# A hybrid decoder step on one core: the place of a weight split, the order and places of filler matmuls, and the reload of x

## What is computed

```
h = rms_norm(x); u = h @ w_in                       # RWKV, attention and gate columns
o_r = rwkv_time_mix(u_r); o_f = forgetting_attention(u_f)
merged = sigmoid(g_r) * (o_r @ w_br_rwkv) + sigmoid(g_f) * (o_f @ w_br_fox)
x = x + merged @ w_out
h2 = rms_norm(x); x = x + square(relu(h2 @ w_up)) @ w_down
y = rms_norm(x)
```

```
state = state * w_t - (state @ kk_t) (kk_t * a_t)^T + v_t k_t^T ;  y_t = state @ r_t
```

## Time and profile before

| what | us |
|---|---|
| median of 3 runs | 2137.5 |
| lowest and highest of these | 2125.45, 2142.78 |
| the profiled execution | 2131.06 |
| its span, first to last instruction | 2129.2 |
| PE busy in the span | 2043.7 (96%) |

### The profile page before, as it was taken

How to read it: one execution, slowest core, us unless ns; L and a number is a source line. 1 busy time by engine, 2 the same in 40 slices (tenths; PEclk the granted TensorE clock), 3 DMA queues, 4 the chain that set the end, 5 groups by cost and what they waited for, 6 DMA issues and landing times.

```text
span 2129.2 us, 43171 instructions
## 1 busy us (share of the span) xinstructions
PE 2043.7 (96%) x17718; PEld 1836.3 (86%) x17718; DVE 943.1 (44%) x1507; ACT 617.1 (29%) x997; POOL 194.6 (9%) x186
## 2 busy tenths in 40 slices
PE   7999989999999999998899999999999999999997
PEld 7996678888888887665566999999999999999997
DVE  6557554444444454607685753332123222222334
ACT  5015332322232222214354642322022012202313
POOL 0000222222222222001110000000000000000000
PEclk9999999999999999999999999999999999999999
DMA  4214621111222202746644561111111111111112
GB/s 168 89 30 167 203 54 44 43 33 45 54 64 74 73 29 75 187 98 251 204 157 162 190 223 47 40 50 49 40 50 40 50 45 43 49 39 50 41 48 81
DMA packets 112938, 185.36 MB, mean 87 GB/s; under 512 B 65198, under 2 KB 68590, under 8 KB 111238
## 3 DMA queue, kind: packets, MB, share of 16 engines
q1 hardware_dynamic: 110502, 174.91, 26.2%
q10 hardware_dynamic: 2304, 8.50, 1.5%
HBM read 147.71 MB, written 35.67 MB: 86 GB/s over the span
## 4 chain that ended last, share of the span: by engine, by line
PE 84%; DVE 6%; DMA 4%; SPq 2%; issue 2%; ACT 1%; ACTq 0%; DVEq 0%
PE ps L292 47%; PE ps L385 10%; PE ps L996 4%; PE ps L997 3%; PE ps L381 3%; PE ps L382 2%; PE ps L383 2%; DMA weights<-in_wu 1%; PE ps L1027 1%; SPq L805 1%; DVE arena L1870 1%; PE ps L872 1%; DMA normed<-in_vp 1%; DVE arena L2036 1%; PE ps L1239 1%
## 5 line engine op out<-in xcount | busy, mean ns | idle before, releaser
L292 PE MATMUL ps<-h_high,wb_split 128*128 128x350 f32 x1536 | 290.5, 324 | 0.0
L292 PE MATMUL ps<-ff_high,wb_split 128*128 128x350 f32 x1488 | 281.0, 323 | 0.0
L302 ACT CAST wb_split<-weights 128x1024 fp32r<-128x1024 f32 x88 | 92.1, 1046 | 600.6 <-PE ps L292 592.9
L292 PEld LDWEIGHTS ps<-h_high,wb_split 128*128 128x128 f32 x1536 | 254.7, 189 | 0.4
L292 PEld LDWEIGHTS ps<-ff_high,wb_split 128*128 128x128 f32 x1488 | 247.2, 189 | 0.0
L385 PE MATMUL ps<-normed,weights 128*128 128x350 f32 x696 | 229.1, 477 | 0.0
L385 PEld LDWEIGHTS ps<-normed,weights 128*128 128x128 f32 x696 | 130.3, 194 | 67.7 <-issue 7.3
L2194 DVE TENSOR_TENSOR arena<-arena,ps 128x1050 f32 (+1 forms) x39 | 48.7, 1249 | 314.1 <-PE ps L292 314.1
L2277 POOL TENSOR_TENSOR arena<-arena,constants 64x512 f32<-64x512 f32 x120 | 132.7, 1106 | 386.9 <-DVE arena L1870 325.9
L292 PE MATMUL ps<-ff_low,wb_split 128*128 128x350 f32 x744 | 160.3, 323 | 0.0
L996 PEld LDWEIGHTS ps<-arena 64*64 64x64 f32 x2400 | 145.0, 135 | 16.7 <-issue 15.7
(11 more groups left out here) (329 smaller groups left out, 3406.8 us busy)
## 6 DMA issues: line engine op xcount, KB each, us to landing
weights<-in_wu SPq DMA_DIRECT2D x122, 512.0 KB, 3.5
normed<-in_vp SPq DMA_DIRECT2D x64, 260.0 KB, 4.7
normed<-in_kp SPq DMA_DIRECT2D x64, 256.0 KB, 5.6
arena<-chunk_dram SPq DMA_DIRECT2D x10, 1248.0 KB, 6.9
arena<-gate_dram SPq DMA_DIRECT2D x16, 525.0 KB, 4.1
chunk_dram<-arena SPq DMA_DIRECT2D x12, 520.0 KB, 5.0
chunk_dram<-fox SPq DMA_DIRECT2D x12, 520.0 KB, 4.6
arena<-samp_dram SPq DMA_DIRECT2D x10, 512.0 KB, 9.5
```

The source lines that it names most:

```text
L292: last = pe.matmul(PS[:, 3 * s + g, 0:G], ws[s][wh][:, k * P:(k + 1) * P], tile_of(x[xh], k)[:, g * G:(g + 1) * G], start=(k == 0 and wh + ...
L302: act.copy(of[0][s][0], W[:, s]).then_inc(w_hi[s], 1)
```

## The change

There are three edits. First, in a chunk DVE makes the second side's low weights behind the four masks, where they stood ahead of them. Second, the fillers change in order and place: in every second group (those with an odd number, from chunk 1 on) the 8 tiles run in the opposite order, so 5 to 0 and then 7 and 6, and the first matmul of a group opens the accumulation whichever tile it is; the four fillers that stood behind both rounds of products become two behind each round. Third, SP fetches x in 8 DMAs of one tile, each behind the two gate tiles of a pass of the branch loop, where it was one DMA behind the loop; DVE waits for all eight.

```diff
--- before.py
+++ after.py
@@ -359,8 +359,9 @@
 
             def __init__(self, pe, v, ns=0, first=None):
                 self.pe, self.v, self.ns, self.first = pe, v, ns, first
-                late = [*range(NS, KT), *range(NS)] if ns or first else range(KT)
-                self.left = [(s, g, i, k) for s in range(2) for g in range(NG) for i, k in enumerate(late)]
+                late = [*range(NS, KT), *range(NS)] if ns or first else list(range(KT))
+                self.left = [(s, g, i, k) for s in range(2) for g in range(NG)
+                             for i, k in enumerate(late[::-1] if ns and (NG * s + g) % 2 else late)]
 
             def run(self, n=None):
                 for s, g, i, k in self.left[:n]:
@@ -378,7 +379,7 @@
                     out, w = PS[:, 6 + m % 2, 0:G], W[:, s, k * P:(k + 1) * P]
                     if k < self.ns:
                         wl_ = WL[:, s, k * P:(k + 1) * P]
-                        self.pe.matmul(out, fill_w(s, k), HF[:, k, at], start=False, stop=False)
+                        self.pe.matmul(out, fill_w(s, k), HF[:, k, at], start=(i == 0), stop=False)
                         self.pe.matmul(out, fill_w(s, k), HL[:, k, at], start=False, stop=False)
                         last = self.pe.matmul(out, wl_, HF[:, k, at], start=False, stop=(i == KT - 1))
                     else:
@@ -840,16 +841,24 @@
             reload(V_BR0 + 1, 0)
             sp.wait_ge(da_step, 11)
             sp.wait_ge(o_done, 2)
+            def x_tile(n):
+                sp.dma_start(XT[:, n, :] if isinstance(n, int) else
+                             XT[:, bass.ds(n, 1), :].rearrange("p o n -> p (o n)"),
+                             A["xt"][:, n, :] if isinstance(n, int) else
+                             A["xt"][:, bass.ds(n, 1), :].rearrange("p o n -> p (o n)")).then_inc(x_back, 16)
+
             gates_back(0)
             reload(V_BR0 + 1, 1)
+            x_tile(0)
             sp.wait_ge(sg_ready, 2)
             gates_back(1)
+            x_tile(1)
             with sp.Fori(2, KT) as n:
                 reload(n + V_BR0, 0)
                 reload(n + V_BR0, 1)
                 sp.wait_ge(sg_ready, 2 * n)
                 gates_back(n)
-            sp.dma_start(XT, A["xt"]).then_inc(x_back, 16)
+                x_tile(n)
             with sp.Fori(V_OUT0, PAIRS) as v:
                 for s in range(2):
                     reload(v, s)
@@ -1028,8 +1037,8 @@
                                                  AR[rows, p].rearrange("p a b -> p (a b)"), start=True,
                                                  stop=True)
                         ch_pe.done(last, f"prod_{m}{i}")
-
-                fill.run(4)
+                    fill.run(2)
+
                 wait(ch_dve, "mask_k1")
                 wait(ch_dve, "nat_v")
                 for h, e, p, rows in by_rows():
@@ -1861,8 +1870,6 @@
                 done(dve.tensor_copy(Bn[0:C], PS[0:C, 1, :]), "nat_b")
                 wait(ch_pe, "nat_v")
                 done(dve.tensor_copy(Vn[0:C], PS[0:C, 3, :]), "nat_v")
-                if early:
-                    fill_split_low(dve, c, 1)
                 cm = cst[0:C, C_CM:C_CM + 2 * C].unsqueeze(1).unsqueeze(1).to_broadcast([C, 2, 2, 2 * C])
                 for i in range(2):
                     for m, dst, bank in (("k", MK, 4), ("b", MB, 0)):
@@ -1871,6 +1878,8 @@
                             dst[0:C].rearrange("p (e a) x t -> p e a (x t)", e=2)[:, :, 2 * i:2 * i + 2],
                             PS[0:C, bank:bank + 2, 0:4 * C].rearrange("p e (a n) -> p e a n", a=2),
                             cm, ALU.mult), f"mask_{m}{i}")
+                if early:
+                    fill_split_low(dve, c, 1)
                 wait(ch_pool, "bm_0_low")
                 done(dve.tensor_tensor(XTr[0:C], identP[0:C].unsqueeze(1).to_broadcast([C, NH, HB]),
                                        Bm[0][0:C], ALU.subtract), "xt_init")
@@ -2184,7 +2193,7 @@
                                   MGS[0][:, tile, :].rearrange("p o n -> p (o n)"), ALU.subtract).then_inc(mg_split, 1)
                 dve.wait_ge(mg_split, n + 1)
 
-            dve.wait_ge(x_back, 16)
+            dve.wait_ge(x_back, 16 * KT)
             order(dve.memset(norms[1][1], 0.0))
 
             def residual(j, unit, s):
```

## The result

The new kernel took 2108.36 us (median of 5 runs, 2105.12 to 2110.54) against 2136.42 for the kernel before (median of 5, 2125.45 to 2142.78): a ratio of 0.9878 (estimated over all runs, so not quite the quotient of the medians; likewise below), 95% interval 0.9842 to 0.9914. The forecast was 2107. Its profiled execution took 2109.26 us with a span of 2107.4, which is 21.8 us less than the span before. This is where they lie; a stretch ends where PE's next stage begins.

The account below looks back on a forecast made before the run. TensorE, busy for 96% of the span, was taken as the bound. Gains of 6.7 (x), 3.8 (chunks 1 to 4), 12.9 (chunks 5 to 9) and 0.8 (chunk 0) make 24.2 us off 2131.06: 2107 us, range 2095 to 2122.

Parts of the forecast that it names:

- Which places: PE loses time between each chunk's two rounds, waiting for DVE's masks, and 6.66 us at the output projection's start.
- x by tiles: Branch loop into output projection: fetching x by tiles removes the 4.72 us stall and slow clock behind it, gaining 6.66 us.
- without a gap: Branch loop: PE was said to run through it with no gap, the cover against later weight loads.
- the lateness that the prediction feared in each pass: Branch loop: an x tile delays each weight load by up to 2.51 us, within the 2.87 us free.
- the rival of a slower loop: Branch loop: x tiles hold up each weight load beyond 2.87 us, at worst 2201 us in total; chance 0.05.
- What is late next: Chunks, before `t1` of level 1: PE waits a new 0.8 us for POOL's `bm_1`, delayed by the split beside it.
- I take the whole 1.03 us: Chunks: the low-weight split beside POOL was priced at its full length, 1.03 us, on POOL's chain before `t1`.
- The clock: Chunks 5 to 9: the clock no longer falls, so each gains 2.57 us, 12.9 in all.
- The rival with the clock lost in all nine: Chunks: the clock falls at the new wait before `t1`, 1.61 us in all nine, giving 2121.6 us; chance 0.20.
- the prediction's guess: Chunks: the profiled execution lies 6.4 us below the median, perhaps because four more chunks lose their clock in other runs.
- sharing costs nothing: Rival, chunks: the split costs POOL nothing, PE doesn't wait, 0.8 us more in each of nine, 2100 us; chance 0.14.
- The order of groups: Fillers in chunks: opposite order shifts slots by 0.22 us, bounded at 2 us either way; taken as zero.

Follow-up runs that it names:

- the second profile of the kernel after: The kernel after run once more with no edit, on the chip of the last three experiments; 2102.41 us (4 runs), ratio 0.9847.
- the forward order: The kernel after without its second edit's opposite order, so all groups of fillers run forward; 2105.33 us (4 runs), ratio 0.9855.

## Why the prediction held, point by point

**Which places.** Both were the right ones. Behind the change PE has no wait for the masks, the masks follow the copy of v, the two rounds stand two tiles apart, and the output projection follows the branch loop without a gap.

**x by tiles.** Forecast 6.66 us; the two stages together are 6.8 us shorter with this edit alone and in the second profile of the kernel after, and 7.6 in the first. The 0.8 more isn't x's: PE has two waits for DVE in the loop's first pass (0.55 and 0.39 us in the kernel before, which the prediction's "without a gap" passed over), and the first profile after is the only trace without them. Of the lateness that the prediction feared in each pass, one case is there, in the second pass of that profile: a copy of weights by ScalarE waits 0.47 us for the load behind an x tile. In the later passes, and in the other six traces with x by tiles, there is none, and PE has no gap behind the first pass, so the rival of a slower loop is out. (ScalarE issues 16 bulk DMAs of its own, but they start between 859 and 967 us in the kernel before; in the branch loop SP's list is the only one.)

```profile
1177.73 1.05 ACT L302 CAST wb_split<-weights 128x1024 fp32r<-128x1024 f32 x1 [0.47 <-DMA weights<-in_wu]
```

**What is late next.** The chain was right: POOL is the new wait before `t1`, in nine chunks, and it comes from the split beside it. Shown by taking the split away (no wait, 57.99 us) and by moving it behind `bm_1` (the price goes with it, 58.01 us).

**The mis-sized term: "I take the whole 1.03 us".** POOL's four instructions took 5.59 us, so the split cost them 0.57, and PE's wait was 0.57 us where 0.8 was forecast. That is 0.46 us per chunk too dear, about all of the 0.40 by which the chunk (58.48) beat the forecast (58.88). (The wait shrank by only 0.23, since PE, too, came to `t1` about 0.2 us sooner than counted.) The trace of before had the right price, and the prediction passed over it: of such a pair it read DVE's side (L1875) and not POOL's. Two rows of GpSimd in chunk 2 of the kernel before, of one shape; the second has DVE's `xt_init` (L1875, 512 columns) beside it, and the first nothing:

```profile
367.71 1.28 POOL L2277 TENSOR_TENSOR arena<-arena,constants 64x512 f32<-64x512 f32 x1 [9.17 <-DVE arena L1870]
...
370.01 1.78 POOL L2277 TENSOR_TENSOR arena<-arena,constants 64x512 f32<-64x512 f32 x1
...
369.96 0.69 DVE L1875 TENSOR_TENSOR arena<-arena 104x512 f32<-104x512 f32 x1 [2.33 <-POOL arena L2277]
```

So 512 columns on DVE cost POOL 0.50 us, not 0.69. For 768 columns that gives 0.75 at most, less what falls between POOL's instructions, and 0.57 was measured. What misled were the earlier trace rows: they show DVE held off, and what DVE loses is not what POOL loses. Chunk 0 of the same trace has the other order. There POOL's third instruction starts 0.03 us ahead of `xt_init` and loses nothing, `xt_init` takes 1.78 us, and POOL's fourth, a short one, starts beside the rest of it and takes 1.19 us, not 0.86:

```profile
242.62 1.27 POOL L2277 TENSOR_TENSOR arena<-arena,constants 64x512 f32<-64x512 f32 x1
...
243.97 1.19 POOL L2277 TENSOR_TENSOR arena<-arena,constants 40x320 f32<-40x320 f32 x1
...
242.65 1.78 DVE L1875 TENSOR_TENSOR arena<-arena 104x512 f32<-104x512 f32 x1 [2.39 <-POOL arena L2277]
```

One reading fits these rows and those of the kernel after: a POOL instruction loses what is left of DVE's when it begins, less 0.12 to 0.16 us. Left were 0.64 us (chunk 2), 0.46 (chunk 0), and 0.65 and 0.21 beside the two of the split; lost were 0.50, 0.33, 0.49 and 0.09. No kernel was made to test it.

The Trainium skill ("SBUF — State Buffer", section "Who interferes with whom") was weighed in the prediction: that two such instructions exclude each other agrees with the trace, where DVE's second split instruction took 1.49 us instead of 0.42. That the issue order decides who blocks agrees as well, by chunks 0 and 2 above; the swap of DVE's own two instructions is no test of it, since DVE starts ahead of POOL in both. That the split is paid in full, as the prediction drew from that rule, doesn't hold here: it was 0.57 of 1.03 us.

**The clock.** The forecast let five chunks get their clock back, 1.61 us each. They did: chunks 5 to 8 gained 2.96 us, which is 1.34 and 1.62. (The rival with the clock lost in all nine comes to 2121.5 by its own sum, 2107 + 9 x 1.61, not 2121.6.) That the new wait of 0.57 us doesn't lower it is shown too: in the eight traces with the wait for the masks shortened or gone, none of 72 chunks (1 to 9) lost the clock, against five and one of nine in the two traces that keep that wait whole. But the six of 18 lie mostly in one execution, so how often the old code loses it can't be had from two traces. Chunk 0 stands apart: in seven of the ten traces, with old code and new, it lost the clock near its end, at 1.4 to 1.6 us; the two traces of the table above both kept it. The runs say that it varies: the kernel before had mean clocks from 0.983 to 0.992 in its 21 runs beside the experiments, and the kernel after from 0.990 to 0.994 in nine. This agrees with the prediction's guess that the profiled execution of before was better than its median for that reason. Among those 21, clocks of 0.987 and 0.988 (the profiled execution had 0.987) go with 2129.89 to 2132.33 us, and 0.984 and 0.985 with 2133.95 to 2136.96. That it is the chunks that make the difference was not shown, since no trace of a slower run exists.

**What wasn't in the forecast.** The attention, +5.9 us in one profile and -0.3 in the other, at clocks of 0.93 and 0.97: an execution's own, in code that is untouched. And 1.0 us came back between chunk 9 and the scores (0.4 in the second trace): PE waits 1.3 us for DVE's `normed` (L1956 there) in these two traces and in that of the forward order, and in none of the other seven. These three are also the traces whose clock is 1.00 over the whole of that stretch; in the seven it fell shortly ahead of that place (0.80 from 839.77 to 848.50 us in the kernel before), so that PE came there later. The first profile has another wait there, 0.76 us for a load of weights. All this is read from traces and was not tried.

**The sum.** Without the attention's 5.9 us the profile would have given 2131.06 - 21.8 - 5.9 = 2103.4, so the forecast of 2107 was some 3.5 us too high by its own steps: 3.5 of chunks (nine times about 0.39), and 0.9 in the branch loop and output projection, less the 1.0 that came back. That the first median, 2108.36, lies so near to 2107 is therefore in part luck: chunks priced too dear and a slow attention cancel, at least in the one of these runs that has a trace. The second set, 2102.41, is the one that the steps explain. So the case that came true lies between the forecast and its rival "sharing costs nothing" (2100).

**The order of groups.** Taken as zero, and measured as 0.04 to 0.05 us a chunk, some 0.4 in all.

## What to carry to other kernels

Before pricing two engines side by side, look in the old trace for two rows of one shape, one with such a neighbour and one without: their difference is the price, and the neighbour's length is only a bound; see, too, which of the two started first. Cover a wait with work that stands ready on the waiting engine before rearranging the engine that it waits for: here that alone brought 1.18 of 1.34 us, and the rearrangement mostly traded one wait for another until it was put where nobody waits. A large transfer at the end of a loop is better cut up and sent along with the loop's own loads, when each has some us to spare (2.87 here).

## What was unexpected of the hardware

- **The same chunk code lost TensorE's clock in five of nine chunks in one execution and in one of nine in another**, behind the same waits of about 1.5 us; a lost clock cost 1.61 us of a chunk.
- **What DVE's products of two SBUF tensors cost POOL goes by less than their length**: 0.50 us for 0.69, and 0.57 for the pair of 0.69 and 0.42, which alone take 1.03. With the short one first it was the same, 5.58 us for the four against 5.59. Where POOL started 0.03 us ahead, it was DVE's instruction that grew, from 0.69 to 1.78 us, and POOL's next one lost 0.33.
- **The attention's length moved by 8.4 us over ten traces** (204.13 to 212.56) with its clock, at unchanged code.
